# Splitting turned attention weights on GpSimd as well as on VectorE, in a streaming encoder step

## The chip, the cores and the metric

One core of one Trainium2 chip runs the whole program. The metric is the device time of one execution in microseconds. The kernel before took 1271.04 us, the median of three runs (1265.55 to 1272.1).

## The reference

One layer of an encoder trunk over 2048 prompt frames and 64 decoded frames, model width 1024. One input projection feeds 8 attention heads of 64 and a pooling mixer; both are gated, go through one output projection, and a final RMS norm follows. The change concerns the attention of the prompt and of the decoded frames, the gate, and the output projection:

```python
s = einsum('bqhd,bkhd->bhqk', qi, k) * sc + (Fi[..., None] - Ft[..., None, :])
s = where(kpos <= qpos, s, -inf)
pr = softmax(s, axis=-1)
attn = einsum('bhqk,bkhd->bqhd', pr, v)
z = concatenate([attn * silu(ag), pool * silu(pg)], axis=-1)
x = x + gate * (z @ w_out)
```

All is in fp32. TensorE works on fp32r operands, so the kernel writes a number as a high part (rounded to fp32r) and a low part (the number less the high part), and adds the products.

## The kernel before

`stage_project` makes the projections and writes keys, queries, values and gate inputs to scratch memory. `stage_finish` does attention and the output projection. Attention runs head by head; a head is three steps (`STEP_GROUPS`): query columns 0 to 1023 with the decoded frames, then 1024 to 1535, then 1536 to 2047.

A step consists of four kinds of work. *Scores*: for a block of 128 query rows and up to 512 keys TensorE makes two matmuls (L1465, L1466) and, for the last block of a row, adds the mask with a third (L1468), into one of three PSUM banks `sps`. VectorE copies the block to SBUF (`wts`) and keeps the running maximum (L1603), and after a row's last block makes the negated maximum (L1608). *Exponentials*: ScalarE, in place on pieces of up to 1024 keys, with the sum of each piece (L1541). *Units*: a unit is one tile of 128 keys times up to 512 query columns. TensorE turns its four 128x128 tiles (L1481) into one of three PSUM banks `tps`. ScalarE writes the high part `whi` (L1547), VectorE the low part `wlo` (L1613), each with six buffers, and TensorE multiplies the values by both (L1496) into `ops`. Units on the diagonal leave out the columns that the mask would make zero. *Out*: a group of units ends in ScalarE's copy of one half (L1555) and VectorE's sum into `att` (L1621).

The row sums of a step are added up (L1629) and inverted on VectorE (L1632, L1633, "den"), written to scratch memory by `rec_out` on SP (L1360, L1363), and read back spread over partitions by `gate_in` (L1375), with the gate inputs (L1373). GpSimd multiplies gate and reciprocal (L1706), makes the high part of the gated attention output (L1711), the same in fp32 (L1712), and the low part (L1715); `gate_out` writes both parts to scratch (L1385). This is done once a pair of heads, for the steps of the second one, in two sets of buffers, each part asking for the part before the last to be done.

The output stage takes 17 tiles of tokens: TensorE multiplies the gated outputs by the output weights' high and low parts (L1516 to L1518); ScalarE makes the high parts (L1531), VectorE the eight low ones (L1595), both while attention ends.

Every engine works in order. The order is made on the host by the class `Plan`, which plays the work forward: each kind has a function `ready` (when its inputs and buffers are there), a cost and a latency in ns, and of all the work that can begin the earliest is taken, ties going by a fixed order (`PRIORITY`). TensorE, ScalarE and VectorE go through the resulting lists; GpSimd and SP follow lists that the code spells out. Semaphores hold back what comes too early: before, a turn waits until the low part of the unit three before it is made, since that reads the same bank.

## Time and profile before

| | before |
|---|---|
| median of three runs | 1271.04 us |
| the profiled execution | 1271.73 us |
| its span | 1269.9 us |
| TensorE busy (matmuls) | 1231.5 us, 97% |
| VectorE busy | 714.3 us, 56% |
| ScalarE busy | 565.9 us, 45% |
| GpSimd busy | 185.3 us, 15% |
| mean granted TensorE clock | 0.989 of full speed |

The shares are means over the three stages (projections, attention, output), which differ. Matmuls overlap in the array, and each is shown with its own whole duration, so a stretch in which TensorE is busy all the time can still hold short waits; the distance from one start to the next is what a matmul costs. A view by stretches gives for each stretch its bounds and length in us, then the busy time (and the number of instructions) of PE, PEld, DVE, ACT and POOL, the granted clock, and the share and GB/s of the DMA engines. PE is TensorE's matmuls, PEld its weight loads, DVE VectorE, ACT ScalarE, POOL GpSimd and SPq SyncE's DMA queue.

### The profile page before, as it was taken

To read this page: it belongs to the slowest core of one execution; us is meant where nothing else is said; L and a number is where in the kernel's file an instruction comes from. 1 tells how busy PE (TensorE), PEld (TensorE's weight loads), DVE (VectorE), ACT (ScalarE), POOL (GpSimd) and SP (SyncE) were. 2 spreads that over 40 slices of the span, in tenths; PEclk is the share of its full clock that TensorE was granted. 3 is DMA by queue.
4 is the path that set the end of the run, shared out by engine and by line. 5 is a ranking of instruction groups with operands and counts; after the bars stand their busy time and mean duration, and the time that the engine had idled before them with its cause. 6 is when DMAs were issued, how large, how long until landed. Compare 5 with 4: busy or idle time off the path is not lost. (4 is left out here: it accounts for less than half of the span.)

```text
span 1269.9 us, 19390 instructions
## 1 busy us (share of the span) xinstructions
PE 1231.5 (97%) x7023; PEld 1029.5 (81%) x7023; DVE 714.3 (56%) x1974; ACT 565.9 (45%) x1163; POOL 185.3 (15%) x193
## 2 busy tenths in 40 slices
PE   5899999999999999999999999999999998999997
PEld 1799988888888888888878788877877876888886
DVE  1756433333564121110059899999999999444444
ACT  3756321222121111211158788887888878111111
POOL 1433301010010100101000051032013106100000
PEclk9899999999999999999989999999999999999999
DMA  9856454022122344347174759849777875666663
GB/s 365 321 174 189 144 152 141 34 69 83 36 85 69 135 147 137 112 128 182 53 166 41 148 95 162 120 103 178 100 136 137 90 188 148 190 203 199 199 199 100
DMA packets 162037, 179.52 MB, mean 141 GB/s; under 512 B 34789, under 2 KB 124265, under 8 KB 157782
## 3 DMA queue, kind: packets, MB, share of 16 engines
q1 hardware_dynamic: 157174, 161.24, 51.2%
q10 hardware_dynamic: 4768, 17.04, 4.1%
q8 instruction: 57, 0.93, 0.3%
q14 instruction: 38, 0.31, 0.2%
HBM read 111.55 MB, written 66.69 MB: 140 GB/s over the span
## 5 line engine op out<-in xcount | busy, mean ns | idle before, releaser
L617 PE MATMUL prj_acc<-prj_hhi,til_whi 128*128 128x512 f32 (+1 forms) x800 | 285.9, 357 | 0.0
L618 PE MATMUL prj_acc<-prj_hhi,til_wlo 128*128 128x512 f32 (+1 forms) x800 | 284.8, 356 | 0.0
L619 PE MATMUL prj_acc<-prj_hlo,til_whi 128*128 128x512 f32 (+1 forms) x800 | 283.7, 355 | 0.0
L1603 DVE TENSOR_SCALAR_CACHE_REDUCE att_wts<-att_sps 128x512 f32<-128x512 f32 (+4 forms) x328 | 186.7, 596 | 92.3 <-PE att_sps L1468 90.9
L1613 DVE TENSOR_TENSOR att_wlo<-att_tps,att_whi 128x512 fp32r<-128x512 f32 (+1 forms) x336 | 183.5, 584 | 17.9 <-ACT att_whi L1547 17.1
L1547 ACT ACTIVATE att_whi<-att_tps 128x512 fp32r<-128x512 f32 (+1 forms) x336 | 160.8, 516 | 53.1 <-PE att_tps L1481 28.5
L1541 ACT ACTIVATE att_wts<-att_wts,att_nm 128x1024 f32<-128x1024 f32 (+8 forms) x200 | 175.2, 880 | 16.6 <-DVE att_nm L1608 14.3
L617 PEld LDWEIGHTS prj_acc<-prj_hhi,til_whi 128*128 128x128 f32 x800 | 150.5, 188 | 22.0
L619 PEld LDWEIGHTS prj_acc<-prj_hlo,til_whi 128*128 128x128 f32 x800 | 150.5, 188 | 21.6
L618 PEld LDWEIGHTS prj_acc<-prj_hhi,til_wlo 128*128 128x128 f32 x800 | 150.6, 188 | 21.0
L1481 PE MATMUL att_tps<-keep_ident,att_wts 128*128 128x128 f32 x1088 | 159.9, 277 | 7.5 <-DVE att_wlo L1613 6.8
L1481 PEld LDWEIGHTS att_tps<-keep_ident,att_wts 128*128 128x128 f32 x1088 | 126.1, 142 | 37.4 <-issue 19.2
L1496 PE MATMUL att_ops<-att_whi,att_vt 128*128 128x512 f32 (+1 forms) x336 | 136.8, 412 | 0.9 <-DVE att_wlo L1613 0.5
L1496 PE MATMUL att_ops<-att_wlo,att_vt 128*128 128x512 f32 (+1 forms) x336 | 120.0, 365 | 0.0
L977 DVE SCALAR_TENSOR_TENSOR til_olo<-prj_acc,til_ohi 128x512 fp32r<-128x512 f32 (+1 forms) x40 | 23.8, 598 | 153.4 <-ACT til_ohi L800 153.3
L530 POOL TENSOR_TENSOR til_wlo<-til_wraw,til_whi 128x1024 fp32r<-128x1024 f32 x20 | 48.1, 2404 | 410.2 <-ACT til_whi L726 410.2
L1706 POOL TENSOR_TENSOR att_ag<-att_ag,att_rb 128x512 f32<-128x512 f32 (+1 forms) x20 | 22.1, 1106 | 398.3 <-DMA att_rb<-scratch_rden 398.3
L1567 ACT ACTIVATE zin_junk<-zin_y 128x1024 bf16<-128x1024 f32 (+1 forms) x16 | 16.9, 1058 | 140.2 <-DVE zin_y L1648 140.2
L1496 PEld LDWEIGHTS att_ops<-att_whi,att_vt 128*128 128x128 f32 x336 | 65.1, 194 | 9.2 <-DVE att_wlo L1613 2.3
L1465 PE MATMUL att_sps<-keep_ka,keep_qa 128*128 128x512 f32 (+4 forms) x164 | 67.3, 410 | 1.6 <-PEq L203 1.5
L1496 PEld LDWEIGHTS att_ops<-att_wlo,att_vt 128*128 128x128 f32 x336 | 64.7, 193 | 4.2
L1465 PE MATMUL att_sps<-att_ka,att_qa 128*128 128x512 f32 (+4 forms) x164 | 66.0, 402 | 0.0
(202 smaller groups left out, 1861.4 us busy)
## 6 DMA issues: line engine op xcount, KB each, us to landing
til_wraw<-in_w_in SPq DMA_DIRECT2D x20, 512.0 KB, 4.1
scratch_v<-val_vs SPq DMA_DIRECT2D x17, 512.0 KB, 4.7
val_xt<-in_x_prompt ACTq DMA_DIRECT2D x16, 512.0 KB, 4.5
ini_al<-in_w_ada SPq DMA_DIRECT2D x8, 1024.0 KB, 15.7
zin_zh<-scratch_z SPq DMA_DIRECT2D x16, 512.0 KB, 4.3
zin_zl<-scratch_z SPq DMA_DIRECT2D x16, 512.0 KB, 5.8
zin_xr<-in_x_prompt SPq DMA_DIRECT2D x16, 512.0 KB, 5.5
out_y_prompt<-zin_o ACTq DMA_DIRECT2D x15, 512.0 KB, 2.7
```

The costliest lines, as they stand in the source:

```text
L530: pool.tensor_tensor(wlo[t.n % 2][:, :, :], wraw[:, :, :], raw(whi[t.n % 2][:, :, :]), ALU.subtract).then_inc(wt_lo, 1)
L617: pe.matmul(out, w[0][:, k, :], hhi[:, k, cs], start=(k == 0), stop=False)
L618: pe.matmul(out, w[1][:, k, :], hhi[:, k, cs], start=False, stop=False)
L619: mm = pe.matmul(out, w[0][:, k, :], hlo[:, k, cs], start=False, stop=(k == KT - 1))
L977: dve.scalar_tensor_tensor(out=olo[use.slot][:, 0:x.n], in0=acc[x.i % ACC_RING][:, 0:x.n], scalar=SCALE if x.tile.kind == "Q" else 1.0, in ...
L1465: pe.matmul(bank[0:x.m, 0:x.n], qa[e][:, q], ka[e][:, k], start=True, stop=False)
L1481: mm = pe.transpose(bank[:, t * P:(t + 1) * P], weights(st, 4 * x.c + t, x.w0, P), keep["ident"][:, :])
L1496: mm = pe.matmul(bank[:, x.skip:x.width], vt[e][0:x.keys, x.tile, :], part[b][0:x.keys, x.skip:x.width], start=(x.first and part is whi), ...
L1541: act.activation(w, w, ACT.Exp, bias=nm[0:x.m, e, x.row:x.row + 1], accum_out=den[0:x.m, e, x.row, x.part:x.part + 1]).then_inc(exp_ok, 1)
L1547: act.activation(whi[x.i % W_RING][0:x.keys, x.skip:x.width], tps[x.i % T_RING][0:x.keys, x.skip:x.width], ACT.Copy).then_inc(hi_ok, 1)
L1603: dve.tensor_scalar(weights(st, x.row, x.w0, x.n), sps[x.i % S_RING][0:x.m, 0:x.n], 1.0, None, ALU.mult, ALU.max, accum_out=top[0:x.m, e, ...
L1613: dve.tensor_tensor(wlo[b][0:x.keys, x.skip:x.width], tps[x.i % T_RING][0:x.keys, x.skip:x.width], raw(whi[b][0:x.keys, x.skip:x.width]), ...
```

## The change

- VectorE no longer makes the low part of every unit. Units in `POOL_UNITS` (index 3 modulo 4, not of the decoded frames, no columns left out, not in the last step) are copied by ScalarE in fp32 to one of two buffers `wf`; GpSimd makes the high part from that by a copy and then the low part by a subtraction. The turn that reuses the bank waits for ScalarE's copy instead of the low part.
- GpSimd's work gets its place from `Plan` too. Its gate operations are planned no earlier than 11 us after the reciprocals of the following step (for the last head: of their own step). For these, SP fetches the inputs after the following step's `rec_out`.
- Reciprocals: `rec` has 32 columns for each of three steps, is turned by VectorE in blocks of 32x32 and written in four DMAs per step, in rows of 32 numbers. The addresses in `rden` leave a place for the decoded frames.
- Of the eight low parts of the output weights VectorE makes four and GpSimd four.
- `Plan` ranks a score on TensorE by how many of the score banks are still full, puts values ahead of it otherwise, and counts a matmul as 0.9 ns a column and pair where it was 6/7.
- The mask stays a matmul on TensorE.

```diff
+F_UNITS = 2
+W_DVE = KT // 2
+POOL_UNITS = [u.i for u in UNITS if u.i % 4 == 3 and not u.dec and not u.skip and u.step.index < len(STEPS) - 1]
+GATE_LAG = 11000
+def gate_step(st):
+    return st.index + (st.head < HEADS - 1)
...
-    PRIORITY = {"PE": ("turn", "score", "value"), "ACT": ("out", "high", "exp", "w_high"), "DVE": ("low", "add", "score", "den", "w_low")}
+    PRIORITY = {"PE": ("turn", "value", "score"), "ACT": ("out", "high", "exp", "w_high"), "DVE": ("low", "add", "score", "den", "w_low"),
+                "POOL": ("p_high", "p_low", "g_lo", "g_z", "g_hi", "g_mul", "w_plow")}
...
         if kind == "high":
+            if x.i in POOL_UNITS:
+                r = POOL_UNITS.index(x.i)
+                return max(at("turn", x.i), at("p_low", POOL_UNITS[r - F_UNITS]) if r >= F_UNITS else 0)
             return max(at("turn", x.i), at("value", x.i - W_RING))
+        if kind == "p_high":
+            return max(at("high", x.i), at("value", x.i - W_RING))
+        if kind == "g_mul":
+            return max(at("add", x.i), at("den", gate_step(x.step)) + GATE_LAG)
...
-            return 24 + 6 * x.n // 7 + mask + (80 if self.short else 0), 200
+            return 24 + 9 * x.n // 10 + mask + (80 if self.short else 0), 200
+        if kind == "w_plow":
+            return 2400, 150
+        if engine == "POOL":
+            return (650 if kind == "p_high" else 1300 if kind == "p_low" else 30 + 5 * x.width // 2), 130
...
+    def rank(self, engine, kind, x, t):
+        if engine != "PE" or kind != "score":
+            return self.PRIORITY[engine].index(kind)
+        waiting = sum(self.at("copied", i) > t for i in range(max(0, x.i - S_RING), x.i))
+        return -1 if waiting < 1 else 0.5 if waiting < 2 else 2
...
         def rec_out(sp, st):
-            sp.wait_ge(rec_ok, st.index + 1)
-            h, e, r = st.head, st.e, st.rows
-            sp.dma_start(dram["rden"][h, P * r.start:P * r.stop].rearrange("(t p) -> p t", p=P),
-                         rec[:, e, r], allow_slow_non_contiguous=True).then_inc(rd_out[e], 16)
-            if 0 in st.groups:
-                sp.dma_start(dram["rden"][h, SEQ:T].rearrange("(p t) -> p t", t=1), rec[0:DEC, e, NQ:NR]).then_inc(rd_out[e], 16)
+            sp.wait_ge(rect_ok, st.index + 1)
+            h, e, r, first = st.head, st.e, st.rows, 0 in st.groups
+            at = rec_at(P * r.start)
+            for b in range(4):
+                n = r.stop - r.start + (first and b < 2)
+                dst = dram["rden"][h, at:at + P * n].rearrange("(t b c) -> b t c", b=4, c=32)[b]
+                sp.dma_start(dst, rec_t[32 * b:32 * b + n, st.index % NG, :]).then_inc(rd_out[st.index % NG], 16)
...
                 rec_out(sp, st)
+                if st.index and STEPS[st.index - 1].e == 1 and gate_step(STEPS[st.index - 1]) == st.index:
+                    gate_in(sp, STEPS[st.index - 1])
...
-                if st.e == 1:
+                if st.e == 1 and gate_step(st) == st.index:
                     gate_in(sp, st)
...
                     pe.wait_ge(exp_ok, need + 1)
-                    if x.i >= T_RING:
-                        pe.wait_ge(lo_ok, x.i - T_RING + 1)
+                    if x.i - T_RING in POOL_UNITS:
+                        pe.wait_ge(hi_ok, x.i - T_RING + 1)
+                    elif x.i >= T_RING:
+                        pe.wait_ge(lo_ok, dve_units(x.i - T_RING))
...
-                    pe.wait_ge(lo_ok, x.i + 1)
+                    if x.i in POOL_UNITS:
+                        pe.wait_ge(p_ok, POOL_UNITS.index(x.i) + 1)
+                    else:
+                        pe.wait_ge(lo_ok, dve_units(x.i))
...
+                elif kind == "high" and x.i in POOL_UNITS:
+                    r = POOL_UNITS.index(x.i)
+                    act.wait_ge(t_full, x.i + 1)
+                    if r >= F_UNITS:
+                        act.wait_ge(p_ok, r - F_UNITS + 1)
+                    act.activation(wf[r % F_UNITS][:, :], tps[x.i % T_RING][:, :], ACT.Copy).then_inc(hi_ok, 1)
...
+                    dve.reciprocal(rec[:, at, 0:n], den[:, e, r, 0]).then_inc(rec_ok, 1)
+                    dve.wait_ge(rec_ok, x.index + 1)
+                    dve.transpose(rec_t[:, at, :], rec[:, at, :]).then_inc(rect_ok, 1)
...
+                    if kind == "p_high":
+                        pool.wait_ge(hi_ok, x.i + 1)
+                        if x.i >= W_RING:
+                            pool.wait_ge(val_ok, x.i - W_RING + 1)
+                        pool.tensor_copy(whi[b][:, :], wf[r % F_UNITS][:, :]).then_inc(p_hi, 1)
+                    else:
+                        pool.wait_ge(p_hi, r + 1)
+                        pool.tensor_tensor(wlo[b][:, :], wf[r % F_UNITS][:, :], raw(whi[b][:, :]), ALU.subtract).then_inc(p_ok, 1)
...
+                if kind == "w_plow":
+                    pool.wait_ge(w_hi, x.i + 1)
+                    pool.tensor_tensor(o_lo[:, x.i, :], o_raw[:, x.i, :], raw(o_hi[:, x.i, :]), ALU.subtract).then_inc(w_plo, 1)
```

## Rows read from the trace of the kernel before

**Rows 1.** Busy time by stretch: the three stages.

```profile
0.00:644.00 644.00, 622.08 (x3655) 537.75 (x3655) 222.20 (x575) 179.95 (x321) 95.28 (x113) 0.99 0.42 136
644.00:1081.00 437.00, 428.13 (x2569) 342.00 (x2570) 404.80 (x1222) 358.95 (x784) 84.39 (x76) 0.98 0.74 132
1081.00:1270.00 189.00, 181.34 (x800) 149.77 (x798) 87.27 (x178) 26.99 (x58) 5.60 (x4) 0.99 0.59 180
```

**Rows 2.** The chain that ended last: start us, us, what.

```profile
829.49 1.31 PE att_tps L1481 x12
...
862.78 2.17 PE att_ops L1496 x12
...
914.96 2.15 PE att_ops L1496 x12
...
970.02 2.15 PE att_ops L1496 x12
```

**Rows 3.** Busy time by stretch: one head, and the last 8 us of attention.

```profile
760.00:812.00 52.00, 51.87 (x322) 41.97 (x321) 48.64 (x152) 43.91 (x97) 5.13 (x4) 1.00 0.83 130
...
1073.00:1081.00 8.00, 5.70 (x25) 4.21 (x24) 8.00 (x9) 3.80 (x6) 5.25 (x3) 0.79 1.13 317
```

**Rows 4.** TensorE in order of time: start us, us, engine, line, operation.

```profile
846.12 0.40 PE L1496 MATMUL att_ops<-att_wlo,att_vt 128*128 128x512 f32 x1
846.35 0.40 PE L1496 MATMUL att_ops<-att_whi,att_vt 128*128 128x512 f32 x1
```

**Rows 5.** Groups of instructions: busy us, mean ns | idle before them.

```profile
L1481 PE MATMUL att_tps<-keep_ident,att_wts 128*128 128x128 f32 x1088 | 159.9, 277 | 7.5 <-DVE att_wlo L1613 6.8
...
L1613 DVE TENSOR_TENSOR att_wlo<-att_tps,att_whi 128x512 fp32r<-128x512 f32 x211 | 136.4, 682 | 17.5 <-ACT att_whi L1547 17.1
```

**Rows 6.** GpSimd: two groups over the span, one operation in order of time.

```profile
L530 POOL TENSOR_TENSOR til_wlo<-til_wraw,til_whi 128x1024 fp32r<-128x1024 f32 x20 | 48.1, 2404 | 410.2 <-ACT til_whi L726 410.2
...
L518 POOL CAST keep_identb<-keep_ident 128x128 bf16<-128x128 f32 x1 | 0.3, 291 | 0.1
...
848.67 1.30 POOL L1706 TENSOR_TENSOR att_ag<-att_ag,att_rb 128x512 f32<-128x512 f32 x1 [4.19 <-DMA att_rb<-scratch_rden]
```

**Rows 7.** GpSimd and VectorE at one time; L1613, ns min/median/max.

```profile
1052.87 1.29 POOL L1715 TENSOR_TENSOR att_zlo<-att_rb,att_zhi 128x512 fp32r<-128x512 f32 x1
...
1053.22 0.69 DVE L1613 TENSOR_TENSOR att_wlo<-att_tps,att_whi 128x512 fp32r<-128x512 f32 x1
...
L1613 DVE TENSOR_TENSOR att_wlo<-att_tps,att_whi x336: 207/680/694, 654.5 to 1079.4; 128x512 fp32r<-128x512 f32 x120, 128x256 fp32r<-128x256 f32 x24, 128x64 fp32r<-128x64 f32 x8, 128x384 fp32r<-128x384 f32 x8
```

**Rows 8.** Row sums (L1629), ns min/median/max; rows in order of time.

```profile
L1629 DVE TENSOR_TENSOR att_den<-att_den x16: 153/156/1236, 687.1 to 1059.6; 128x4 f32<-128x4 f32 x16
...
1059.52 1.27 POOL L1706 TENSOR_TENSOR att_ag<-att_ag,att_rb 128x512 f32<-128x512 f32 x1 [3.88 <-DMA att_rb<-scratch_rden]
...
1059.58 1.24 DVE L1629 TENSOR_TENSOR att_den<-att_den 128x4 f32<-128x4 f32 x1 [1.11 <-ACT att_wts L1541]
...
848.54 1.86 DVE L1613 TENSOR_TENSOR att_wlo<-att_tps,att_whi 128x512 fp32r<-128x512 f32 x3
```

**Rows 9.** Output weights (L1595), ns min/median/max; GpSimd beside one.

```profile
L1595 DVE TENSOR_TENSOR olo_w<-raw_w,ohi_w x8: 1208/1363/2092, 1063.6 to 1081.1; 128x1024 fp32r<-128x1024 f32 x8
...
1063.58 2.36 POOL L1715 TENSOR_TENSOR att_zlo<-att_rb,att_zhi 128x512 fp32r<-128x512 f32 x1
```

**Rows 10.** Waits of GpSimd (655 to 1056) and SP: us, times, longest.

```profile
POOL att_ag L1706 <- DMA att_rb<-scratch_rden: 374.6, 13, 128.5
...
SPq L1372 <- DMA scratch_rden<-att_rec: 70.7, 11, 12.1
```

**Rows 11.** TensorE at the end of attention, in order of time.

```profile
1062.62 0.63 PE L1481 MATMUL att_tps<-keep_ident,att_wts 128*128 128x128 f32 x4 [2.06 <-DVE att_wlo L1613]
...
1076.58 0.73 PE L1481 MATMUL att_tps<-keep_ident,att_wts 128*128 128x128 f32 x4 [1.81 <-DVE att_wlo L1613]
...
1080.81 0.40 PE L1516 MATMUL att_sps<-ohi_w,zin_zh 128*128 128x512 f32 x1
```

More of the change, by code:

```diff
@@ L1697, in _ @@
         def _(pool):
[L1698 to L1715 removed]
+            pool.memset(rec[:, :, :], 0.0).then_inc(rec_zero, 1)
```

115 lines of the change are left out of this document (70 added, 45 removed).

## The prediction, made before the changed kernel was run

> **What bounds the kernel now.** I read the stages first. The projections take 644 us of the span and the output stage 189 us, and the change touches neither, except for the weights that the output stage uses first. The attention stage takes 437 us, and there TensorE is busy for 428 us, VectorE for 405 us and ScalarE for 359 us [rows 1]. A busy TensorE is not a full one, because matmuls overlap, so the second view is one head at a time. The same burst of twelve value matmuls returns after 52.2 us, in one head after 55.1 us [rows 2]; the shorter distance stands for the heads. In 52 us VectorE is busy for 48.6 us (93%) and ScalarE for 43.9 us (84%) [rows 3].
>
> How long would TensorE need for a head if it never waited? The reader takes the distance from start to start where work is back to back: 0.23 us for a 512-column value or score matmul [rows 4], and 1.31/12 = 0.109 us for a turn [rows 2]. A head has 136 turns (1088/8 [rows 5]): 14.8 us. Its 42 units are 28 of 512 columns, four each of 384, 256 and 128, and two of 64, every one twice (high and low part): by columns 2 x (28 x 0.23 + 12 x 0.115 + 2 x 0.03) = 15.8 us. The score blocks are 28, 12 and one more by the same count, also twice: 15.9 us. The 17 masks I put at 0.06 us each, an estimate from the 0.23 us of 512 columns for 128: 1 us. Together 47.5 us of 52.2. So TensorE waits about 4.7 us in a head, in many small pieces, while VectorE waits only 3.6 us. The two are coupled by three PSUM rings of scores and turned tiles, and VectorE is the fuller one. Relief for VectorE should therefore show, but not beyond 4.7 us a head.
>
> **The weights split.** Every unit with index 3 modulo 4 that is full, not of the decode rows and not in the last step goes to GpSimd: counting by the unit table, 49 of 336. Each takes one 512-column subtraction (L1613) from VectorE. Such a one lasts 0.682 us, and three in a row take 1.86 us, so one is worth 0.61 us [rows 5, 8]. Removed: 49 x 0.61 = 30 us of VectorE. ScalarE's copy keeps its size and only writes to another buffer. The turn three units later is released by the copy and no longer by the subtraction, which is earlier.
>
> GpSimd gets 49 copies and 49 subtractions. The subtraction is priced by its present ones of that size, 1.29 us. For a 512-column copy there is no row: 128x128 casts and selects take 0.29 us, and a 512-column two-input operation takes 1.29 us, so the bounds are 0.3 and 1.3 us; I take 0.65, twice the small one, because it should stay under the two-input form [rows 6]. A unit's GpSimd work is then 1.9 us (1.6 to 2.6), and at four units in about 5 us (52.2/42 = 1.24 us for one) GpSimd has room. All this lies beside other work. Its price is the delay: from the turn to a usable low part it takes ScalarE's 0.6 us (an estimate: as VectorE's of the same size), 0.65 and 1.29 us and three handovers of 0.1, 2.8 us, against 1.4 us now. The ring of six weight buffers covers six units, over 7 us, if the order has the value matmuls that late.
>
> **Do VectorE and GpSimd hinder each other?** The trace has both answers. While GpSimd runs a 1.29 us operation at 1052.87, VectorE's subtraction at 1053.22 takes its usual 0.69 us, and the longest of all 336 took 0.694 [rows 7]. It reads one PSUM and one SBUF tensor. The sum of the row parts (L1629) with both inputs in SBUF takes 0.156 us at the median and 1.236 us when it begins 0.06 us after a GpSimd operation: it waits for that one's end [rows 8]. The output weights (L1595), also two SBUF inputs, go from 1.21 to 2.09 us, and GpSimd's own operations beside them from 1.29 to 2.36 us [rows 9]. The Trainium skill says (SBUF — State Buffer, section "Who interferes with whom") that a VectorE instruction with two SBUF inputs contends with a GpSimd one that reads SBUF, and that one with at most a single SBUF input outside the two-port modes doesn't. By that rule the moved work is clean; the trace agrees. The same skill (Perfetto Trace Analysis, section "Optimizing Scalar/DVE Operations") warns that moving work between these two might not help because of that port; taken at its word it would leave no gain at all. The row on L1613 speaks against it.
>
> What collides is L1629, 16 times in the stage. GpSimd is busy some 40% of the time after the change, so each pays on average 0.4 x 0.6 = 0.25 us: 4 us (0 to 16 x 1.1 = 17 us).
>
> **Turned reciprocals.** Added on VectorE: 24 transposes of 128x32 and a wait for the reciprocal just before each. The transpose has no row; a small VectorE operation takes 0.156 us [rows 8] and a 512-column one 0.61, so 0.2 to 0.6 us each with its wait; I take 0.25, near the small one: 6 us (5 to 14). Removed are DMAs that scatter single numbers: SP waited 70.7 us for these writes in 11 pieces [rows 10]. Added are four issues of rows of 32 numbers, at some 0.4 us each. Nobody but the gate path waits for either, so in the heads this is worth nothing on the critical path; if SP's queue were late with the next head's keys it would cost, and the trace shows no such wait on TensorE.
>
> **The gates.** For heads 1, 3 and 5 their inputs are fetched after the next step's reciprocals, and GpSimd's products are ordered another 11 us later. On SP they pass one reciprocal write and stand ahead of the loads of values and keys. Now GpSimd waits 374.6 us in front of its first gate operations [rows 10], which costs nothing, since nothing was queued behind. After the change split units are queued behind. The first gates of a step should find their data. The third of a step can't be fetched before the first is done (two buffers); that was a wait of 4.19 us [rows 6], and it comes once a pair of heads: 4 x 0 to 4 us on the split units, part of it hidden by the ring. I take 2 us in all.
>
> **The output weights.** Four of the eight low parts go to GpSimd. VectorE spent eight times 1.36 us (the median), 11 us, on them between 1063.6 and 1082 [rows 9]; the last ones stand ahead of subtractions for which TensorE waits 1.81 us at 1076.58, and its granted clock in those 8 us is 0.79 on average, against 1.00 in the heads [rows 3, 11]; after a long wait it falls from 2.4 to 1.2 GHz for some us. Without them that wait and some of the low clock go: 3 us of gain (0 to 5). The wait of 2.06 us at 1062.6 [rows 11] comes from L1629 behind the last exponentials and the GpSimd lock; it can return. GpSimd's four of 1024 columns take 2.4 us each [rows 6], some 10 us beside four gate operations; TensorE needs the last of them 42 matmuls of 0.23 us, 9.7 us, after it begins the output stage at 1080.8 [rows 4, 11], so this is just covered, and uncovered it costs up to 4 us.
>
> **The sum.** VectorE's net relief: 30 - 6 - 4 = 20 us over eight heads, 2.5 a head. TensorE's floor of 47.5 allows it (52.2 - 2.5 = 49.7), but at 96% full not all can show; I take three quarters, 15 us, and 2 off for the gates' wait: 13. The planner's new rule (values ahead of scores, unless the score ring runs empty) and its corrected matmul cost may remove the excess of the longer head, 55.1 - 52.2 = 2.9 us: 2 of it. With 3 us at the end: 18 us. The profiled execution took 1271.7 us, of which 1269.9 are its span and 1.8 lie around it; it is 0.7 above the median of 1271.0. Forecast: 1271.7 - 18 = 1254 us.
>
> **Rivals.** *GpSimd is late.* It works in order, and a split unit behind a 1.29 us gate operation, a fetch or a slow copy (1.3 us) gets its low part after TensorE wants it. TensorE also works in order: turns and scores behind that value matmul wait too, and VectorE then starves. With lateness d on each of 49 units the loss is 49 d; it beats the gain of 18 us from d = 0.37 us on. With a 1.3 us copy and a planned margin of under half a microsecond d is 0.65 us: +32 - 18 = +14 us, 1286; half of the units late gives 1269. For it: only four of the planner's GpSimd costs rest on present rows, and orders are fixed. Against: the ring of six and 60% idle time. Chance 0.17 for a time above 1277.
> *VectorE isn't the limit.* TensorE's small waits come from the fixed order and from ScalarE at 84%; then only the end's gain stays, eaten by the locks: 1271.7 - 3 + 2 = 1271. For it: no long wait of TensorE for L1613 stands in the heads. Against: VectorE at 93%. Chance 0.15, also for the case that lateness and relief cancel.
> *The locks and the transposes cost their upper bounds.* 30 - 14 - 17 gives no relief in the heads, and 3 + 2 stay elsewhere: 1267. Chance 0.08.
> *The whole gap closes.* The new order brings heads near 48.3 us, 0.8 above the floor: 8 x 3.9 + 3 = 34 us, 1238. Chance 0.12.
> *The forecast's case*, 1244 to 1262: chance 0.48.
>
> **How the numbers follow.** A measurement of this kernel can tell about 0.5%, 6 us. Faster by more than that: 0.48 + 0.12 + 0.08 = 0.68; within: 0.15; slower: 0.17. The range leaves out half of the whole-gap case and most of the late-GpSimd case above 1277: 1241 to 1277 us.
>
> **What would show it.** Right: heads return every 49.5 to 50.5 us; VectorE's busy share in them falls to about 90%; L1613 counts 287 and keeps 0.68 us; the copy takes about 0.65 us on GpSimd; the output stage begins near 1063. Wrong: TensorE or its weight loads waiting for GpSimd's subtraction for more than some 5 us in total; L1629 at 1 us on average; heads still at 52 us with an emptier VectorE; TensorE waiting in the first output token for GpSimd's weights.

## The result, and the profile after

The changed kernel takes 1304.4 us (median; 1302.3 to 1306.5), the kernel before 1271.4 us beside it: ratio 1.027, 95% interval 1.0235 to 1.0305. It is 33 us slower, where 17 us less were forecast. The profiled execution took 1302.3 us.

Busy time by stage shows where (the line of column names, then the three stages as in [rows 1]):

```profile
core 0: us, PE busy (x) PEld busy (x) DVE busy (x) ACT busy (x) POOL busy (x), PEclk, DMA share, GB/s
0.00:644.00 644.00, 620.96 (x3657) 536.88 (x3657) 222.20 (x575) 180.29 (x322) 95.39 (x114) 0.99 0.42 137
644.00:1110.00 466.00, 431.45 (x2563) 343.87 (x2562) 387.96 (x1193) 359.38 (x784) 182.69 (x178) 0.96 0.53 126
1110.00:1301.00 191.00, 183.00 (x806) 150.82 (x804) 85.34 (x177) 27.10 (x59) 6.96 (x5) 0.99 0.56 171
```

The attention stage is 466 us long instead of 437. VectorE did get its relief: 388 us busy in it, from 405. But TensorE, with the same work, now stands still for 35 us there (9 us before), and its granted clock is 0.96 (0.98 before). The slices of the whole span show both, in three places (each digit one fortieth of the span, 32.5 us):

```profile
PE   4899999999999999999999979997999897999997
PEclk8899999999999999999999998998999899999999
```

The first wide dip is the slice from 748 to 780 us. Its waits are these, from the table of waits of the attention stage (engine, tile, line, releaser: us, times, longest):

```profile
POOL att_ag L1792 <- DMA att_rb<-scratch_rden: 81.0, 15, 14.9
ACT att_whi L1613 <- PE att_ops L1554: 45.0, 36, 8.1
DVE att_wlo L1679 <- ACT att_whi L1613: 39.3, 29, 7.3
PE att_ops L1554 <- POOL att_wlo L1781: 24.2, 6, 7.4
```

24.2 us of TensorE waiting for GpSimd's subtraction, nearly all of it in three waits: 7.37 us at 782.75, 6.61 at 898.18 and 7.08 at 1014.14. ScalarE and VectorE wait behind TensorE. GpSimd's timeline before the first of them:

```profile
762.12 0.61 POOL L1778 CAST att_whi<-att_wf 128x512 fp32r<-128x512 f32 x1
762.81 1.28 POOL L1781 TENSOR_TENSOR att_wlo<-att_wf,att_whi 128x512 fp32r<-128x512 f32 x1
778.45 1.26 POOL L1792 TENSOR_TENSOR att_ag<-att_ag,att_rb 128x512 f32<-128x512 f32 x1 [14.36 <-DMA att_rb<-scratch_rden]
779.65 0.61 POOL L1778 CAST att_whi<-att_wf 128x512 fp32r<-128x512 f32 x1
780.22 1.26 POOL L1798 TENSOR_TENSOR att_zhi<-att_ag,att_att 128x512 fp32r<-128x512 f32 x1
781.44 1.26 POOL L1781 TENSOR_TENSOR att_wlo<-att_wf,att_whi 128x512 fp32r<-128x512 f32 x1
```

GpSimd stands for 14.36 us before the first product of a gate, whose reciprocals (att_rb) haven't landed. The copy and subtraction of a split unit are queued behind; TensorE gets the low part at 782.7:

```profile
782.75 0.80 PE L1554 MATMUL att_ops<-att_whi,att_vt 128*128 128x512 f32 x1 [7.37 <-POOL att_wlo L1781]
```

Why the reciprocals are late stands on the queue of SyncE:

```profile
755.67 1.14 SPq L193 DMA_DIRECT2D att_qa<-scratch_q  x2
756.85 1.24 SPq L193 DMA_DIRECT2D att_ka<-scratch_k  x2
760.81 0.30 SPq L193 DMA_DIRECT2D att_kb<-scratch_fkd  x1
...
762.57 0.34 SPq L1424 DMA_DIRECT2D att_ag<-scratch_ag  x1
762.96 1.09 SPq L1426 DMA_DIRECT2D att_rb<-scratch_rden  x2
```

The fetch (L1424, L1426) is issued at 762.6 to 764.1, right behind the keys and queries of the head after next: ten transfers, of which the six large ones are 528 and 560 KB each, 3.3 MB together. It takes until 778. Its time from issue to landing is at the median 3.2 us over the kernel, and 15.0 at most. The same thing comes at 893.87 (14.64 us) and 1009.83 (14.92 us): the last gates of heads 1, 3 and 5, those whose keys load stands in front.

After each of these stalls the clock is down: here around the first and the third.

```profile
773.00:783.00 10.00, 2.63 (x18) 2.02 (x17) 3.31 (x10) 2.99 (x8) 4.55 (x5) 0.73 1.09 208
784.00:788.00 4.00, 4.00 (x19) 3.48 (x19) 2.49 (x5) 1.42 (x3) 2.96 (x3) 0.53 0.05 8
788.00:798.00 10.00, 9.93 (x59) 7.84 (x58) 8.89 (x29) 9.16 (x18) 1.91 (x2) 1.00 0.01 3
1010.00:1020.00 10.00, 5.86 (x24) 5.04 (x24) 2.76 (x7) 1.79 (x3) 8.53 (x9) 0.50 0.67 105
```

TensorE was busy for 2.6 of 10 us, and then runs at 0.5 (1.2 GHz) and later at 1.00 (2.4 GHz) again. To see what a stall costs in all, I took the start of every fourteenth low-part value matmul (counted from 0) from both traces, after minus before: it goes from +1.3 us to +12.0 between the 84th and the 98th, from +12.2 to +22.5 between the 168th and the 182nd, from +20.5 to +31.2 between the 252nd and the 266th. Three times some 10.5 us. In the stretches between, it falls: by 1.2 us from the 98th to the 154th, by 3.1 from the 182nd to the 238th, by 2.6 from the 266th to the 322nd. That is no gain of the change: the new order puts the value matmuls elsewhere within a head, so this distance moves without any stall too. The clean price of a stall needs a kernel with the same order and no stall, which is e1 below.

The moved work itself is as priced (x: count; busy us, mean ns), apart from the sum of the row parts, which was [rows 8] before:

```profile
L1781 POOL TENSOR_TENSOR att_wlo<-att_wf,att_whi 128x512 fp32r<-128x512 f32 x49 | 62.8, 1283 | 2.6
L1778 POOL CAST att_whi<-att_wf 128x512 fp32r<-128x512 f32 x49 | 29.9, 609 | 194.6 <-ACT att_wf L1608 146.9 <-PE att_ops L1554 47.7
L1679 DVE TENSOR_TENSOR att_wlo<-att_tps,att_whi 128x512 fp32r<-128x512 f32 x173 | 114.5, 684 | 39.8 <-ACT att_whi L1613 38.5
L1693 DVE TENSOR_TENSOR att_den<-att_den 128x4 f32<-128x4 f32 x16 | 5.7, 357 | 1.2 <-ACT att_wts L1601 1.1
L1705 DVE STREAM_TRANSPOSE att_rec_t<-att_rec 128x32 f32<-128x32 f32 x24 | 5.1, 212 | 0.8
```

### The profile page after: what moved, and what is told of

It reads as the page before. It is cut to its first block and busy times, and to the rows that moved or that the text cites. A ratio compares the mean times of both kernels' runs of the same rounds, so it can differ in the third digit from the quotient of the medians.

```text
span 1300.6 us, 19610 instructions
## 1 busy us (share of the span) xinstructions
PE 1235.4 (95%) x7023; PEld 1031.6 (79%) x7023; DVE 695.5 (53%) x1945; ACT 566.8 (44%) x1163; POOL 285.0 (22%) x296
## 5 line engine op out<-in xcount | busy, mean ns | idle before, releaser
L1601 ACT ACTIVATE att_wts<-att_wts,att_nm 128x1024 f32<-128x1024 f32 (+8 forms) x200 | 175.5, 881 | 23.3 <-DVE att_nm L1674 22.5
L1679 DVE TENSOR_TENSOR att_wlo<-att_tps,att_whi 128x512 fp32r<-128x512 f32 (+5 forms) x287 | 155.0, 568 | 43.6 <-ACT att_whi L1613 41.9
L1536 PE MATMUL att_tps<-keep_ident,att_wts 128*128 128x128 f32 x1088 | 162.9, 281 | 10.0 <-DVE att_wlo L1679 6.6
L1613 ACT ACTIVATE att_whi<-att_tps 128x512 fp32r<-128x512 f32 (+5 forms) x287 | 136.0, 501 | 68.2 <-PE att_ops L1554 45.0
L1554 PE MATMUL att_ops<-att_whi,att_vt 128*128 128x512 f32 (+1 forms) x336 | 137.5, 413 | 24.4 <-POOL att_wlo L1781 24.2
L1778 POOL CAST att_whi<-att_wf 128x512 fp32r<-128x512 f32 x49 | 29.9, 609 | 194.6 <-ACT att_wf L1608 146.9
```

Of the source, the lines that this page charges most:

```text
L1536: mm = pe.transpose(bank[:, t * P:(t + 1) * P], weights(st, 4 * x.c + t, x.w0, P), keep["ident"][:, :])
L1554: mm = pe.matmul(bank[:, x.skip:x.width], vt[e][0:x.keys, x.tile, :], part[b][0:x.keys, x.skip:x.width], start=(x.first and part is whi), ...
L1601: act.activation(w, w, ACT.Exp, bias=nm[0:x.m, e, x.row:x.row + 1], accum_out=den[0:x.m, e, x.row, x.part:x.part + 1]).then_inc(exp_ok, 1)
L1613: act.activation(whi[x.i % W_RING][0:x.keys, x.skip:x.width], tps[x.i % T_RING][0:x.keys, x.skip:x.width], ACT.Copy).then_inc(hi_ok, 1)
L1679: dve.tensor_tensor(wlo[b][0:x.keys, x.skip:x.width], tps[x.i % T_RING][0:x.keys, x.skip:x.width], raw(whi[b][0:x.keys, x.skip:x.width]), ...
```

## The experiments

All ratios are to the kernel before, measured beside each version on the same chip. Its median there was 1268.9 to 1270.2 us. A distance between two medians can differ by 2 to 3 us from what the ratios give. My theory after the traces: 28 of the 33 us are the fetch behind the keys. The rivals: GpSimd is late by itself, and the planner's new orders are worse.

### The fetch behind the keys

**e1.** The keys and queries of the head after next are issued one step later for the odd heads, behind the fetch:

```diff
-                if at == NG - 1 and st.head + 2 < HEADS:
+                if at == 0 and st.e == 0 and st.index:
+                    done = STEPS[st.index - 1]
+                    sp.wait_ge(s_full, done.blocks[-1].i + 1)
+                    load_qk(sp, dram, qk[1], done.head + 2, qk_in[1])
+                if at == NG - 1 and st.e == 0 and st.head + 2 < HEADS:
```

> One edit to the changed kernel, on SP alone: the keys and queries that are loaded after an odd head's last scores (for head + 2) are issued one step later, behind the fetch of that head's last gate inputs instead of ahead of it. Every engine's order stays. Theory A (the fetch waits in the DMA queue behind 2.2 MB of keys and queries, GpSimd waits for it in order, and the split units behind it stop TensorE): the three waits of 14.4 to 14.9 us of GpSimd (before 778, 894, 1010) fall to under 4 us, TensorE's three waits of some 7.4 us for GpSimd and the three stretches of 10.2 us at half the clock go; at 10.5 us each the time is 1304 - 31 = 1273 us (1266 to 1276). Theory B (GpSimd's split is too slow or too late everywhere, and the fetch only coincides): under 10 us come back, 1294 us or more.

Measured: 1275.9 us, ratio 1.0064 (1.0042 to 1.0086). In its trace the fetch lands after 6.5 us at the latest:

```profile
DMA to landing us min/median/max: 2.3/3.1/6.5
```

TensorE's waits for GpSimd's subtraction fall from 24.2 to 2.0 us. GpSimd still waits 14.3 us once, at 1044, for the first gate of the last head, but TensorE doesn't wait for GpSimd there. (My text above gives the keys and queries as 2.2 MB; they are 3.3.)

The engines of e1 go through exactly the lists (the planned order of each engine's work) of the changed kernel, so the starts of the same value matmuls give the price of the stalls. The changed kernel minus e1 is -2.5 us at the 84th and +6.7 at the 98th, +6.8 at the 168th and +15.6 at the 182nd, +15.7 at the 252nd and +24.9 at the 266th, and +24.9 at the last. The three stalls cost 9.1, 8.7 and 9.2 us, 27 together, and between them the two kernels keep step.

**e10.** The same with less moved: within the step, the order on the queue is fetch, keys, gate results.

```diff
+                if st.index % NG == NG - 1 and st.head + 2 < HEADS:
+                    sp.wait_ge(s_full, st.blocks[-1].i + 1)
+                    load_qk(sp, dram, qk[1], st.head + 2, qk_in[1])
                 if n >= 1:
                     gate_out(sp, n - 1)
...
```

> The changed kernel, new order, with the same issue order on SP: fetch, keys, writes. Engines' orders as in the changed kernel. Theory A holds with the keys only 1 us behind the fetch as well: as the kernel with the keys moved, 1276 us (1272 to 1279). If the fetch is still overtaken or slowed by the keys behind it in the same queue, one or more of GpSimd's waits stays over 8 us and the time is 1285 or more.

Measured: 1277.3 us, 1.0062 (1.0039 to 1.0085). The fetch lands after 5.8 us at most. The gate results, now issued behind the keys, are late in its place: up to 16.0 us from issue to landing, where e1 has 6.3.

**e2.** The queue stays, but GpSimd's gates are planned 30 us behind the sums instead of 11, except in the last head (GATE_LAG = 30000).

> One number of the changed kernel: the gate operations of heads 1, 3 and 5 are planned no earlier than 30 us after the next step's reciprocals instead of 11 us; head 7 keeps 11. SP's queue stays, so the fetch is as late as before, only GpSimd gets to it later. Theory A: the same three waits go, since the data is there when GpSimd comes to it, 1273 us (1266 to 1278); all engines' planned orders shift a little, which may cost or bring 3 us. Theory B: 1290 us or more. If this comes out well above the kernel with the keys moved, the plan's place of the gates has a price of its own.

Measured: 1282.0 us, 1.0104 (1.0078 to 1.013). TensorE's waits for GpSimd's subtraction are 0.6 us in all, yet it waits 3.1 us once for keys and still loses its clock once. (Only GpSimd's list changed: the lists of the other three engines came out the same as in the changed kernel.)

Against the kernel before, the change is 33 us slower, e1 6, e10 7 and e2 13: three edits, two on SP's queue and one on GpSimd alone, take 20 to 27 of the 33 us away. The late fetch ahead of split units is the main cause, and that is shown. What is left is 6 us or more over the kernel before; by the value matmuls, e1 loses 4 of them in the first two heads.

### The planner's new orders

**e3.** The changed kernel without any split unit: POOL_UNITS = [].

> The changed kernel with an empty list of split units: VectorE makes the low parts of all 336 units again; gates, turned reciprocals, planner rules and the output weights' halves stay. Theory A: GpSimd still waits 14 us for the fetch three times, but nothing of TensorE is behind it, so the three stops go. What is left against the kernel before is the rest of the change. If the split's relief of VectorE is worth its 15 us in the heads, this kernel stands at 1273 + some 10 = about 1283 us; if the relief is worth little (VectorE isn't the limit) it stands near 1271 to 1275. Theory B: near 1271 as well, but then the kernel with the keys moved stays above 1290.

Measured: 1278.6 us, 1.0075 (1.0047 to 1.0102). With nothing on GpSimd that TensorE waits for in the heads, it is still slower than before. e1, with the split, is 2.7 us faster by the medians, but the two intervals overlap: under these orders no worth of the split is shown.

**e4** and **e12.** The kernel before, with the planner's new rules alone: e4 has all of them (values ahead of scores, the rank by the score ring, the matmul's cost), e12 only the cost, 0.9 ns a column in place of 6/7.

```diff
-            return 24 + 6 * x.n // 7 + mask + (80 if self.short else 0), 200
+            return 24 + 9 * x.n // 10 + mask + (80 if self.short else 0), 200
```

> The kernel before with the planner's new rules alone (values ahead of scores on TensorE unless the score ring runs empty, 0.9 ns a column and pair). No split, old reciprocals, old gates. If the new order is neutral: 1271 us (1268 to 1274). If it removes small waits, as the forecast gave it 2 us: 1269. If it costs, some of the changed kernel's loss is its own: above 1277.

> The kernel before with the planner's matmul cost alone changed (0.9 ns a column and pair for 6/7); turns, scores, values ranked as before. The new rules together cost 9 us. If the cost of a matmul is what does it, 1276 to 1280; if it is the ranks (values ahead of scores), this stays at 1269.5 (1266 to 1273).

Measured: 1278.3 us, 1.0066 (1.0039 to 1.0093), and 1282.8 us, 1.0105 (1.0078 to 1.0132). The rules that I had credited with 2 us cost 9, and one of them alone costs 13. The lists of TensorE, ScalarE and VectorE in e3 and e4 are the same, but for the four low parts of the output weights, and so are the times: what is left in e3 is the order.

**e15.** Is it their direction, or does any new plan scatter? The kernel before with the cost at 0.87 ns a column, 1.5% more than 6/7.

> The kernel before with one number of the planner changed by 1.5 per cent: a matmul's cost 0.87 ns a column in place of 0.857. If a plan's order scatters by itself, the time moves by 5 us or more either way (1260 to 1265 or 1275 to 1283 us). If the 9 to 13 us of the new rules are due to their direction, this one stays within 3 us of the kernel before, 1267 to 1273 us.

Measured: 1280.0 us (1274.5 to 1285.6), 1.0086 (1.0055 to 1.0117). A change of 1.5% in one cost gives another order and 11 us (7 to 15 by the interval; the seven executions of this one order differ by 11 us among themselves). The plan's order is a lottery of this size, and all four new ones without a split (e4 with e3, e12, e15, and e11 below) lie 9 to 13 us above the order of the kernel before. None came out faster; whether the old order was itself picked from many isn't known.

**e5** and **e6.** e1 with the planner's old rules, with the split (e5) and without (e6).

> The kernel with the keys moved, and the planner's rules for TensorE as before (turns, scores, values; 6/7 ns a column and pair; no rank). Split, turned reciprocals, gates' place and the weights' halves stay. The new rules alone cost 9 us on the kernel before (1278.3 against 1269.5). Theory O (the new order costs by itself, whatever the split): 1276 - 9 = 1267 us (1262 to 1270), about 1 to 3 us under the kernel before. Theory P (the new order belongs to the split: values must come earlier in TensorE's order, or the gates fit it): 1276 or more.

> As the last one, with no split units. The difference of the two is what the split is worth under the old order. If VectorE's relief is worth the forecast's 13 us, this is 13 us above the last one, about 1280; if the relief is worth little, the two agree within 3 us. Reciprocals, gates and weights' halves alone should leave it near the kernel before, 1269 us (1267 to 1273).

Measured: e5 1325.8 us, 1.042 (1.0391 to 1.0449); e6 1269.5 us, 1.0001 (0.9978 to 1.0023). e5 says little, for my edit brought a cost of its own: the keys, issued a step later, are now late three times, and TensorE waits 24.1 us for them, beside 10.4 us for GpSimd's subtraction. e6 is clean, for its lists are those of the kernel before, but for the four weights moved to GpSimd: turned reciprocals, the gates' later place and the halved weights change nothing together.

**e9.** e5 without that flaw: the queue order of e10 and the old rules.

> The split under the old order of TensorE, cleanly. The try before (1325.8) was spoiled by its own edit: the keys, issued behind SP's wait for a gate result, landed after TensorE wanted them (it waited 6.5 to 9 us for them three times). Here the fetch of an odd head's last gate inputs is issued first, the keys and queries right behind it, and only then the writes that wait for GpSimd. Gone should be the three waits for keys (about 3 x 12 us with the clock): 1290 us. If the split is harmless under the old order: 1265 to 1270. If it costs there, because values stand earlier behind their turns than GpSimd's chain allows (it waited 10 us for GpSimd in the heads of that try, besides the keys): 1280 to 1300.

Measured: 1304.2 us, 1.0267 (1.024 to 1.0293). So under the planner's old rules the split loses 35 us against e6, with the fetch ahead of the keys. TensorE waits 13.9 us for GpSimd's subtraction in six pieces; one of them has this in front:

```profile
762.04 1.29 POOL L1792 TENSOR_TENSOR att_ag<-att_ag,att_rb 128x512 f32<-128x512 f32 x1 [3.82 <-DMA att_rb<-scratch_rden]
769.91 1.29 POOL L1792 TENSOR_TENSOR att_ag<-att_ag,att_rb 128x512 f32<-128x512 f32 x1 [0.80 <-DMA att_rb<-scratch_rden]
776.25 1.27 POOL L1792 TENSOR_TENSOR att_ag<-att_ag,att_rb 128x512 f32<-128x512 f32 x1 [3.65 <-DMA att_rb<-scratch_rden]
783.05 0.79 PE L1554 MATMUL att_ops<-att_whi,att_vt 128*128 128x512 f32 x1 [3.05 <-POOL att_wlo L1781]
```

Here each gate waits for its inputs only a few us, but every one does, and 5 us of its own work follow. By the value matmuls, 8, 9 and 7 of the 35 us come in the same three stretches as in the changed kernel, behind the last gates of heads 1, 3 and 5. But e9's plan has new orders on all engines, so this alone doesn't say whether the split or the plan is at fault.

### What relief of VectorE is worth

**e8.** The kernel before, with VectorE's subtraction cut to 32 of 512 columns in 44 of the units that the change would move. Most of those units' low parts are left out, so the attention output is not the reference's; everything else, and every order, stays.

```diff
...
+                    width = 32 if x.i in SHORT else x.width
-                    dve.tensor_tensor(wlo[b][0:x.keys, x.skip:x.width], tps[x.i % T_RING][0:x.keys, x.skip:x.width],
+                    dve.tensor_tensor(wlo[b][0:x.keys, x.skip:width], tps[x.i % T_RING][0:x.keys, x.skip:width],
```

> The kernel before, with VectorE's low part cut to 32 of 512 columns in 44 of the units that the change would split (the rest of those low parts keeps old numbers, so the attention output is not the reference's). No GpSimd work, no new wait, same order: VectorE's relief alone, 44 x (0.61 - 0.2) = 18 us. If VectorE is the limit in the heads as forecast, three quarters show: 1269.5 - 13 = 1256 us. If TensorE's small waits come from its fixed order and from ScalarE: within 4 us of before, 1266 or more.

Measured: 1264.6 us, 0.9954 (0.9926 to 0.9981). The removed work is 44 x (684 - 181) ns = 22 us of VectorE:

```profile
L1615 DVE TENSOR_TENSOR att_wlo<-att_tps,att_whi 128x512 fp32r<-128x512 f32 x179 | 118.1, 684 | 26.4 <-ACT att_whi L1548 24.5 <-issue 0.5
L1615 DVE TENSOR_TENSOR att_wlo<-att_tps,att_whi 128x32 fp32r<-128x32 f32 x44 | 8.0, 181 | 0.1
```

5 us of these 22 come out at the end (1269.5 less 1264.6; 2 to 9 by the interval). VectorE's waits for ScalarE grow: 25.7 us for att_whi in this trace, against 17.1 in the kernel before.

**e11.** The same, and the planner is told of the shorter subtractions (98 ns each).

> The relief kernel (VectorE's low part cut to 32 columns in 44 units, output not the reference's) with the planner told so: it counts these low parts at 98 ns where it counted 595, so all three orders are made anew for the relieved VectorE. 18 us of VectorE's work brought 5 us under the old order (1264.5). If the fixed order withheld the rest: 1250 to 1258 us. If TensorE's small waits have another cause (ScalarE at 84%, handovers): 1262 to 1267.

Measured: 1281.4 us, 1.0088 (1.006 to 1.0115). Less work, better told, and 17 us slower than with the old order. The plan again, in two parts by the trace: attention takes 7 us more than in e8, and the first output matmul then waits 8.3 us for the gated outputs of the last head (zin_zl), which GpSimd finishes too late for it.

### The halves of the output weights

**e7** is e1 with the low parts of all eight output weights on VectorE (W_DVE = KT), **e14** is e6 with the same.

> The kernel with the keys moved, and all eight low parts of the output weights on VectorE again, none on GpSimd. In that kernel VectorE's four take 1.2 to 3.4 us each, where one alone takes 1.21, because GpSimd's 2.4 us operations hold them up, and TensorE waits 2.7 us for the last. Theory L (the halves collide and give no gain): the same or up to 3 us faster, 1273 to 1276. The forecast's view (four fewer on VectorE are worth 3 us): 3 us slower, 1279.

> The planner's old rules, no split on GpSimd, turned reciprocals, the gates' new place, and the low parts of all eight output weights on VectorE. If the shared halves of the weights cost something beside GpSimd's gates: 1264 to 1268 us. If they are worth nothing either way: 1268 to 1271 us, as the same kernel with the halves shared out.

Measured: 1275.8 us, 1.0038 (1.0018 to 1.0057), against e1's 1275.9; and 1270.9 us, 1.0003 (0.9984 to 1.0022), against e6's 1269.5. The halves bring no gain; by the ratios of e7 and e1 (1.0038 and 1.0064, with overlapping intervals) a cost of up to 3 us isn't excluded. In the changed kernel three of GpSimd's four end at 1109 and the last at 1111.9, and VectorE's four beside GpSimd's gates last 2.1 us each where eight had 1.5:

```profile
1101.06 8.00 POOL L1785 TENSOR_TENSOR olo_w<-raw_w,ohi_w 128x1024 fp32r<-128x1024 f32 x3 [0.47 <-ACT ohi_w L1591]
```

(from the timeline), and from the groups:

```profile
L1661 DVE TENSOR_TENSOR olo_w<-raw_w,ohi_w 128x1024 fp32r<-128x1024 f32 x4 | 8.5, 2125 | 0.3 <-ACT ohi_w L1591 0.3
```

### The split with every order frozen

**e13.** The orders of TensorE, ScalarE and VectorE are those of the kernel before, written out. Only the split units' copy and subtraction move to GpSimd, in unit order; the queue is that of e10; the weights stay on VectorE.

```diff
...
+    for st in STEPS:
+        for u in st.units:
+            if u.i in gone:
+                pool += [("p_high", u), ("p_low", u)]
+        if st.index and STEPS[st.index - 1].e == 1 and gate_step(STEPS[st.index - 1]) == st.index:
+            pool += [(k, out) for out in STEPS[st.index - 1].outs for k in ("g_mul", "g_hi", "g_z", "g_lo")]
...
```

> The orders of TensorE, ScalarE and VectorE are those of the kernel before, written out; only every fourth unit's split is moved to GpSimd, with the copy and the subtraction in unit order and the gates of a step behind the next step's split units; on the SyncE queue the fetch of a step's gates stands ahead of the keys and queries; all low parts of the output weights stay on VectorE. Theory A (the split is good in itself, only the plan's new orders spoil it): VectorE's relief of 5 us comes through, 1262 to 1268 us. Theory B (the split is bad in itself: copy and subtraction on GpSimd take 1.9 us where VectorE took 0.6, so that the low part comes later than the value matmuls of the old order want it): TensorE waits for GpSimd's subtraction 0.5 to 1.5 us at most of the 49 units, 1285 to 1310 us.

Measured: 1309.9 us, 1.0323 (1.0296 to 1.035). By its number this is my theory B, by its trace it is neither. TensorE waits for GpSimd 33.7 us in six pieces, four of them 7.0 to 9.3 us long, and between them it is as fast as before: its value matmuls keep a distance of 11.3, then 21.5, then 30.5 us to those of the kernel before over 40 to 80 units, with ten or more splits in each stretch. The first of the four:

```profile
746.93 0.32 POOL L1900 TENSOR_TENSOR att_ag<-att_ag,att_rb 128x64 f32<-128x64 f32 x1
753.09 1.26 POOL L1900 TENSOR_TENSOR att_ag<-att_ag,att_rb 128x512 f32<-128x512 f32 x1 [4.62 <-DMA att_rb<-scratch_rden]
757.11 1.26 POOL L1914 TENSOR_TENSOR att_zlo<-att_rb,att_zhi 128x512 fp32r<-128x512 f32 x1
758.31 0.61 POOL L1886 CAST att_whi<-att_wf 128x512 fp32r<-128x512 f32 x1
759.00 1.26 POOL L1889 TENSOR_TENSOR att_wlo<-att_wf,att_whi 128x512 fp32r<-128x512 f32 x1
760.32 0.79 PE L1662 MATMUL att_ops<-att_whi,att_vt 128*128 128x512 f32 x1 [9.27 <-POOL att_wlo L1889]
```

The first step's three gates stand in a row. The third can only be fetched when the first is done (two buffers): 4.62 us, then four operations of 1.26 us, then the split unit, which ScalarE had copied at 749.03.

**e16.** e13 with the gates taken apart, one behind each split unit, the first some eight units into the next step:

```diff
+    for i in POOL_UNITS:
+        pool += [("p_high", UNITS[i]), ("p_low", UNITS[i])]
+        if gates and gates[0].step.units[-1].i + 9 <= i:
+            out = gates.pop(0)
+            pool += [(k, out) for k in ("g_mul", "g_hi", "g_z", "g_lo")]
...
```

> As the kernel with the frozen orders (1309.9 us), with one change on GpSimd: its gates no longer stand three in a row ahead of a split unit, but one behind each split unit, the first some eight units into the step after. Theory A (all that the frozen kernel lost was the row of gates ahead of a split unit, four stalls of 7.7 to 9.5 us and what followed them, while the other 45 splits cost nothing): the four stalls go, 1264 to 1272 us. Theory B (splitting on GpSimd is late by itself, and the gates only gather the lateness in one place): the stalls come back spread out, one to two us at many units, 1285 to 1305 us.

Measured: 1275.0 us, 1.0044 (1.0027 to 1.0061): 35 us less by the place of the gates alone. In its trace TensorE waits for GpSimd 1.3 us in two pieces (0.29 and 1.02), and reaches the last value matmul 6.8 us earlier than before (3.5 of them were there already at the stage's begin). But the first output token has to wait, for the last head's gates are late too:

```profile
1081.32 0.77 PE L1682 MATMUL att_sps<-ohi_w,zin_zh 128*128 128x512 f32 x1 [7.11 <-DMA zin_zl<-scratch_z]
```

**e17.** e16 with the last head's three split units back on VectorE, which leaves 46:

```diff
-POOL_UNITS = [u.i for u in UNITS if u.i % 4 == 3 and not u.dec and not u.skip and u.step.index < len(STEPS) - 1]
+POOL_UNITS = [u.i for u in UNITS if u.i % 4 == 3 and not u.dec and not u.skip and u.step.head < HEADS - 1]
```

> As the frozen kernel with spread gates (1275.0 us), but the last head's three split units go back to VectorE, so that GpSimd does that head's gates as early as in the kernel before. Theory A (the split under unchanged orders gains some 3 us in the attention stage, as the spread kernel's records show up to the last value matmul, and that kernel lost 7 us only at the first output token, whose inputs came late from the late gates): the 7 us go, 1266 to 1269 us, at or a little below the kernel before. Theory B (the attention stage's 3 us belong to the one profiled execution and not to the split): 1270 to 1273 us.

Measured: 1264.8 us (1263.0 to 1266.8), 0.9959 (0.9945 to 0.9972): 5 us below the kernel before, 3% below the changed one, and the first version with the split that beats both. e14 is its twin without the split: the three engines go through the same lists, but for the 46 subtractions. It has 1.0003 against 0.9959 here, so the split is worth 4 to 6 us. Its attention and output stages, cut at the same times as the kernel before's:

```profile
655.00:1081.00 426.00, 418.27 (x2549) 337.50 (x2549) 383.20 (x1174) 350.89 (x767) 173.71 (x172) 1.00 0.56 134
1081.00:1264.00 183.00, 175.92 (x777) 145.37 (x775) 83.96 (x175) 26.40 (x57) 0.83 (x1) 0.99 0.57 175
```

The clock is 1.00 in the stage, and the fetch of the reciprocals (att_rb) has no long landing any more:

```profile
DMA to landing us min/median/max: 2.5/3.2/5.7
```

## Why the prediction was wrong, point by point

**The sign: the gates.** The step that failed is "The first gates of a step should find their data", with the price "I take 2 us in all". I had written myself that the fetch stands ahead of the loads of values and keys. That holds for those of its own step, but the keys of the head after next are issued at the end of the step before, and so directly ahead of the fetch. And I priced only the wait for the two buffers, 4.19 us [rows 6]. The trace of before had the warning that I didn't read: there the fetch att_rb took up to 18.4 us from issue to landing, at a median of 4.0. It was even the same fetch behind the same keys, issued from 753.12 to 759.2, and GpSimd waited longer than it did after the change:

```profile
761.89 0.34 SPq L1373 DMA_DIRECT2D att_ag<-scratch_ag  x1
762.28 1.46 SPq L1375 DMA_DIRECT2D att_rb<-scratch_rden  x2
781.48 1.30 POOL L1706 TENSOR_TENSOR att_ag<-att_ag,att_rb 128x512 f32<-128x512 f32 x1 [21.76 <-DMA att_rb<-scratch_rden]
```

It was harmless as long as nothing stood behind GpSimd's wait. Instead of "4 x 0 to 4 us" on the split units there were three waits of 14.4 to 14.9 us, 7 us of each on TensorE, and 9 us each with the clock: 27 us together, as e1 shows and e10 confirms.

The rival "GpSimd is late" had the right engine and the right sequence, TensorE waiting for a low part in its fixed order. Its working was wrong: it spread a lateness d over 49 units. Nearly all units were in time (1.3 us of lateness in the whole of e16), and a few waited for a transfer. That my price was an average is why 0.17 was too little: an in-order engine loses by its longest wait.

**The size: three quarters of the relief.** That was "15 us" of 20. e8 shows 5 us of 22 (2 to 9 by its interval), e17 5 us of 46 x 0.61 - 5 = 23. It is about a quarter or less in both. VectorE was the fullest engine at 93%, but part of the relief turned into its own waits for ScalarE (8.6 us of the 22 in e8). So of the rivals "VectorE isn't the limit" was nearly right on this step. By the value matmuls of e17 and its twin e14, the split gains 4.0 us in seven heads, 0.6 a head where I had 1.6.

Part of the reason is a term of my floor. I took 0.23 us from start to start for every 512-column matmul, but the first one behind a turn or a mask takes longer. In the kernel before, behind a turn:

```profile
841.90 0.48 PE L1465 MATMUL att_sps<-att_ka,att_qa 128*128 128x512 f32 x1
842.21 0.40 PE L1466 MATMUL att_sps<-att_kb,att_qb 68*128 68x512 f32 x1
842.45 0.40 PE L1496 MATMUL att_ops<-att_whi,att_vt 128*128 128x512 f32 x1
842.68 0.40 PE L1496 MATMUL att_ops<-att_wlo,att_vt 128*128 128x512 f32 x1
```

The first distance is 0.31 us, the third 0.23. Between 656 and 1060 us there are 104 pairs of 512-column value matmuls behind a turn, and all have 0.305 us or more from the first start to the second (median 0.315). e8 and e17 have the same median, so this is a pace of TensorE's own and not a wait that VectorE's relief could shorten. Scores and narrower matmuls show the same. There are some 40 such places in a head, behind a turn or a mask, 3.2 us in all. The floor is then about 47.5 + 3.2 = 50.7 us (an estimate), and what a head of 52.2 us could gain was some 1.5 us and not 4.7: 12 us in eight heads, where I counted on 15. What holds back the rest of these 12 isn't shown. ScalarE waits 49 us for TensorE in the attention stage before, so it isn't shown to be the limit either.

**The planner's rules, "2 of it".** They cost 9 us (e4). I argued from what a rule favours; what came was another draw of the order. The sign can't be argued from the rules, and the bound had to reach some 13 us to the slow side, as e12 and e15 show; no draw was faster. Whether a favourable draw exists with the new rules is open; I didn't look for one.

**The output weights, "3 us of gain".** Nothing (e7, e14). The wait for VectorE's subtractions before the end stayed: in the changed kernel TensorE waits 2.69 us at 1105.12 for L1679, where it waited 1.81. Half of the eight were gone, but the other four took 2.1 us each, for GpSimd's gates ran beside them. (My 11 us for the eight of before were eight medians; together they took 12.1.) That "this is just covered" held: GpSimd was done at 1111.9 and the output stage began at 1111.5.

**Right.** The copy takes 0.61 us (0.65 taken, 0.3 to 1.3 as bounds), the subtraction 1.28, the transpose 0.21 in all 24 (0.25 taken). The full subtraction on VectorE keeps its 0.68 us beside GpSimd, 684 ns in mean over 173, against 682 [rows 5]: the moved work is clean as [rows 7] said. By the rule of the Trainium skill (SBUF — State Buffer, section "Who interferes with whom") it had to be so, and the trace agrees. The sum of the row parts went from 234 to 357 ns in mean, 16 x 0.12 = 2 us (4 taken). Turned reciprocals change no time in the heads (e6). And what would show it wrong was named: TensorE waiting for GpSimd's subtraction for more than 5 us; it was 24.

**The account of the 33 us:** Some 27 for the late fetch (the changed kernel against e1: 26 by the ratios, 27 by the value matmuls), and 6 for what is left in e1. The new orders alone cost 9 (e4, and e3 with the same lists); that the split takes back the other 3 fits, but is within the noise.

## What to carry to other kernels

An engine on whose work nothing urgent depends may wait 15 us without any harm to the time. Before work on the critical path is queued behind it, read the longest landing of each transfer that it waits for, not the median, and see which loads stand ahead of it on the same queue; then keep queued jobs with a DMA behind them apart, one between two critical ones.

Work taken from an engine that is 93% busy gave about a quarter of itself or less at the end. Before such relief is priced, work out the pace of the next engine with all its distances from start to start, those at a change of the kind of work too. And where a planner writes the orders, test an edit with the orders frozen: a 1.5% change of one cost moved this kernel by 11 us, more than everything the edit was worth.

## What the runs showed of the hardware

A fetch of 0.5 MB issued at 762.6 us directly behind 3.3 MB of loads on the same queue landed 14 to 15 us later; issued ahead of them it lands in 6.5 us at most (e1) and 5.8 (e10), though the loads then follow at once. What stands behind the loads is late in its place: up to 16.0 us for the gate results in e10. From 756 to 776 us the DMA engines were busy throughout (share 1.02) and moved 222 GB/s. That makes 4.4 MB, and the keys and queries, the fetch and the gate results behind it are 4.4 MB too by the profile's list of issues. This fits a fetch that waits until what stands ahead of it is moved; by what rule the engines share their work isn't shown.

TensorE was busy until 775.4 us, then idle for 7.4 us. When it began again at 782.75 its granted clock was 0.50 (the low level, 1.2 GHz), and from 788 on it was 1.00 again; the stall of 7.4 us cost 9.1 in all. In e17, where TensorE's stalls in the stage are at most 1.2 us, the stage as a whole has 1.00.

The first 512-column value matmul behind a 128-column turn held TensorE for 0.315 us before the next one started (median of 104), the first one behind a mask as long (0.314, 38), and one behind another value matmul 0.233 (74), in the kernel before from 656 to 1060 us; e8 and e17 show the same.
